# z's last quarter goes into the first rounds of the delta rule; GpSimd makes low parts; the second inverse lives in x's memory

## The reference, cut to what matters

```python
proj = h @ w_in
qkv, z, b_logit, a_logit = jnp.split(proj, ...)
qkv = silu(causal_depthwise_conv(qkv, conv_w))
...
o = chunked_gated_delta_rule(q, k, v, g, beta)      # chunks of 128 tokens, 16 heads
o = rms_norm(o, norm_w) * silu(z)
return o.reshape(bsz, t, GDN_V) @ w_out
```

## Time and profile before

| | us |
|---|---|
| median of 3 runs | 915.18 (913.97 to 915.21) |
| the profiled execution | 915.78 |
| its span, first to last instruction | 913.7 |
| PE busy | 879.3 (96%) |
| DVE busy | 698.0 (76%) |
| ACT busy | 510.4 (56%) |
| POOL busy | 46.6 (5%) |
| mean granted clock of TensorE | 0.977 |

### The profile page before, as it was taken

The page is one execution under the profiler, slowest core; times in us unless marked ns, Lnnn a source line. Parts: engine busy times, 40 slices in busy tenths (PEclk is TensorE's granted clock), DMA queues, the critical chain, the costliest instruction groups (busy, mean ns, idle before and its releaser), DMA issues.

```text
span 913.7 us, 16395 instructions
## 1 busy us (share of the span) xinstructions
PE 879.3 (96%) x6434; PEld 819.8 (90%) x6434; DVE 698.0 (76%) x1116; ACT 510.4 (56%) x729; POOL 46.6 (5%) x48
## 2 busy tenths in 40 slices
PE   5999999989897999999999999999999999999997
PEld 5999998779776999999997899999887799999995
DVE  5777889846756777777757677899999999956874
ACT  6598877546445555555545565333345675435642
POOL 0001110122010000000000000000001130001000
PEclk9999999979998999999999979999999999999999
DMA  8736664610465477777777525555455445555441
GB/s 255 231 116 184 194 178 139 174 53 2 161 208 184 139 251 251 253 248 247 255 248 263 184 77 185 178 184 185 156 173 178 138 139 185 185 190 173 140 143 46
DMA packets 139473, 161.55 MB, mean 177 GB/s; under 512 B 17155, under 2 KB 112283, under 8 KB 139419
## 3 DMA queue, kind: packets, MB, share of 16 engines
q1 hardware_dynamic: 139419, 160.80, 54.3%
HBM read 156.58 MB, written 4.21 MB: 176 GB/s over the span
## 4 chain that ended last, share of the span: by engine, by line
PE 73%; DVE 16%; ACT 5%; issue 2%; DMA 2%; SPq 1%; DVEq 0%; ACTq 0%
PE psum L480 22%; PE psum L482 22%; PE psum L481 22%; DVE w_lo L1376 5%; DVE cv L1819 3%; PE psum L765 3%; DMA w_raw<-in_sc_w_out_dram 1%; ACT w_hi L932 1%; DVE Tq L1604 1%; DVE outer L1602 1%; DVE cacc L1525 1%; PE psum L635 1%; ACT junk L965 1%; PE psum L869 1%; PE psum L647 1%
## 5 line engine op out<-in xcount | busy, mean ns | idle before, releaser
L1376 DVE TENSOR_TENSOR w_lo<-w_raw,w_hi 128x1024 fp32r<-128x1024 f32 x264 | 316.6, 1222 | 129.6 <-ACT w_hi L932 128.4
L932 ACT ACTIVATE w_hi<-w_raw 128x1024 fp32r<-128x1024 f32 x264 | 275.0, 1057 | 213.1 <-PE psum L482 166.6
L480 PE MATMUL psum<-hT_hi,w_hi 128*128 128x256 f32 x1216 | 349.9, 288 | 4.4 <-DVE w_lo L1376 3.8
L481 PE MATMUL psum<-hT_lo,w_hi 128*128 128x256 f32 x1216 | 346.9, 285 | 0.0
L482 PE MATMUL psum<-hT_hi,w_lo 128*128 128x256 f32 x1216 | 346.8, 285 | 0.0
L480 PEld LDWEIGHTS psum<-hT_hi,w_hi 128*128 128x128 f32 x1216 | 236.5, 195 | 5.9 <-issue 4.3
L481 PEld LDWEIGHTS psum<-hT_lo,w_hi 128*128 128x128 f32 x1216 | 236.5, 194 | 0.3 <-issue 0.2
L482 PEld LDWEIGHTS psum<-hT_hi,w_lo 128*128 128x128 f32 x1216 | 236.3, 194 | 0.0
L1819 DVE SCALAR_TENSOR_TENSOR cv<-aP,par,cv 128x256 f32<-128x256 f32 x240 | 106.8, 512 | 0.0
L480 PE MATMUL psum<-w_hi,hT_hi 128*128 128x512 f32 x224 | 91.3, 408 | 1.8 <-DVE w_lo L1376 1.8
L482 PE MATMUL psum<-w_hi,hT_lo 128*128 128x512 f32 x224 | 87.4, 390 | 0.0
(11 more groups left out here) (285 smaller groups left out, 1061.7 us busy)
## 6 DMA issues: line engine op xcount, KB each, us to landing
w_raw<-in_w_in_dram SPq DMA_DIRECT2D x44, 1024.0 KB, 5.0
w_raw<-in_sc_w_in_dram SPq DMA_DIRECT2D x32, 1024.0 KB, 7.3
w_raw<-in_gdn_w_in_dram SPq DMA_DIRECT2D x24, 1024.0 KB, 5.5
ada<-in_w_ada_dram SPq DMA_DIRECT2D x24, 512.0 KB, 4.7
w_raw<-in_gdn_w_out_dram SPq DMA_DIRECT2D x8, 1024.0 KB, 5.4
w_raw<-in_sc_w_out_dram SPq DMA_DIRECT2D x8, 1024.0 KB, 7.3
w_raw<-in_w_ret_out_dram SPq DMA_DIRECT2D x8, 1024.0 KB, 5.1
w_raw<-in_w_conv_out_dram SPq DMA_DIRECT2D x4, 1024.0 KB, 5.1
```

The source lines that it names most:

```text
L480: pe.matmul(o, l_hi, r_hi, start=start, stop=False, skip_group_check=True)
L481: pe.matmul(o, l_hi, r_lo, start=False, stop=False, skip_group_check=True)
L932: act.activation(w_hi[j % 2 * 2 + h][:, :, :], raw[slot][:, h * KH2:(h + 1) * KH2, :], ACT.Copy).then_inc(hi_ready, 1)
L1376: return dve.tensor_tensor(o, whole, hi.bitcast(F32), ALU.subtract)
```

## The change

1. Only chunks 0 to 5 of z run in the z stage (Z_AHEAD). The four halves of chunks 6 and 7 stand ahead of the level products of rounds 0 to 3, into banks 4 and 5; ScalarE's last silu of zo stands at the start of round 4.
2. GpSimd makes w_lo of the second halves of z's chunks 1 to 6 (POOL_LO). Who needs such a half waits for `lo_pool`; VectorE's `lo_ready` skips them and catches up at gdn_out's first half.
3. S[1] moves from w_raw's slot 2 into x's memory, and is cleared once xn is made. SP loads x again after the last V. gdn_out's chunks 2 and 3 are loaded right behind `blocks_home`, the row and chunks 4 and 5 after the last kdec, x, 6 and 7 after the last V.
4. The solve's shares are 10, 12, 12, 12, 16; the turn of its rows 0 to 23 is done before the last share, the other 8 rows after it.
5. k is turned after chunk 0 of z instead of after chunk 5, ahead of v.
6. The splits in the rounds: z's last half in round 0, gdn_out's (0,0), (0,1), (1,0), (1,1) in rounds 1 to 4, (2,0), (2,1), (3,0) in rounds 13 to 15 (before: (1,1) in 12, (2,0), (2,1), (3,0) in 15, 16, 17).

```diff
+SQ_ROWS = 24
-OUT_SPLITS = [(OUT_FROM, 1, 1), (OUT_FROM + 3, 2, 0), (OUT_FROM + 4, 2, 1), (OUT_FROM + 5, 3, 0)]
+Z_AHEAD = 6
+ROUND_SPLITS = [(0, "z", 7, 1), (1, "gdn_out", 0, 0), (2, "gdn_out", 0, 1), (3, "gdn_out", 1, 0), (4, "gdn_out", 1, 1),
+                (OUT_FROM + 1, "gdn_out", 2, 0), (OUT_FROM + 2, "gdn_out", 2, 1), (OUT_FROM + 3, "gdn_out", 3, 0)]
+POOL_LO = range(1, 7)
-        S1 = at("S1", o_raw + 16 * K, [P, VH, P])
+        S1 = at("S1", o_x, [P, VH, P])
...
+        def by_pool(g, h):
+            return h == 1 and g - FIRST["z"] in POOL_LO
+        def low_half(eng, g, h):
+            z0 = FIRST["z"]
+            if by_pool(g, h):
+                eng.wait_ge(lo_pool, g - z0 - POOL_LO[0] + 1)
+            else:
+                others = sum(by_pool(a, 1) for a in range(z0, g)) if g < z0 + COUNT["z"] else 0
+                eng.wait_ge(lo_ready, 2 * g + h + 1 - others)
...
-            for j in (0, 1, 3, 2):
-                if j == 3:
-                    blocks_home()
-                if j == 2:
-                    sp.wait_ge(vn_ready, NPAIR)
-                chunk(FIRST["gdn_out"] + j, j, wide_cols(gdn_w_out[0], j * (KH2 * P), 0))
+            out_chunk(0)
+            out_chunk(1)
+            blocks_home()
+            out_chunk(2)
+            out_chunk(3)
+            sp.wait_ge(kdec_ready, NPAIR)
             sp.dma_start(row[:, :], post_norm_w[0:1, :].to_broadcast([P, D])).then_inc(row_loaded, 16)
-            phase("gdn_out", four_pieces(gdn_w_out[0]), start=1, of=wide_cols)
+            out_chunk(4)
+            out_chunk(5)
+            sp.wait_ge(vn_ready, NPAIR)
+            for t in range(NT):
+                load_x(t)
+            out_chunk(6)
+            out_chunk(7)
...
             for r in range(ROUNDS):
+                if r < 4:
+                    c, h = Z_AHEAD + r // 2, r % 2
+                    if r == 0:
+                        pe.wait_ge(vb_ready, 2 * NPAIR - 1)
+                    wide_half(FIRST["z"] + c, h, 4, hT_hi, hT_lo, c % 2 * KH2, c % 2 == 0, c % 2 == 1)
                 if r < 8:
                     level5_w(r)
...
             for r in range(ROUNDS):
+                if r == 4:
+                    act.wait_ge(half_done, 4 + 2 * FIRST["gdn_out"])
+                    act.activation(zo[:, :, 3 * CW2:4 * CW2], psum[:, 4:6, :], ACT.Silu).then_inc(bank_free, 2)
...
-            pool.wait_ge(lo_ready, 2 * (FIRST["z"] + 7))
+            pool.wait_ge(xn_ready, 2 * NT)
             pool.memset(S[1], 0.0).then_inc(filled, 1)
+            def split_lo(c):
+                g = FIRST["z"] + c
+                s = g % 2 * 2 + 1
+                pool.wait_ge(hi_ready, 2 * g + 2)
+                pool.tensor_tensor(w_lo[s][:, :, :], raw[g % RING][:, KH2:KT, :], w_hi[s][:, :, :].bitcast(F32), ALU.subtract).then_inc(lo_pool, 1)
+            for c in POOL_LO:
+                split_lo(c)
+                if c == 4:
+                    (the memsets of Tc's side and S[0], with their waits)
...
-                    pool.wait_ge(bank_free, 4 + FIRST["gdn_out"])
+                    pool.wait_ge(half_done, 4 + 2 * FIRST["gdn_out"])
...
+            def turn_rows(a, b):
+                return dve.tensor_copy(Lq[:, :].rearrange("p (c r) -> p c r", r=BS)[:, :, a:b], Tq[:, :].rearrange("p (r c) -> p c r", c=BS)[:, :, a:b])
-                solve_share((8, 14, 14, 14, 12, 0, 0, 0)[c])
+                if c == 4:
+                    dve.wait_ge(solve_step, 2 * SQ_ROWS - 1)
+                    turn_rows(0, SQ_ROWS)
+                solve_share((10, 12, 12, 12, 16, 0)[c])
                 if c == 4:
                     dve.wait_ge(solve_step, 2 * (BS - 1) + 1)
-                    dve.tensor_copy(Lq..., Tq...).then_inc(sq_turned, 1)
+                    turn_rows(SQ_ROWS, BS).then_inc(sq_turned, 1)
```

More of the change, by code:

```diff
@@ L237, in build @@
         lnss_ready, ngk_ready, nb_ready = sem("lnss_ready"), sem("ngk_ready"), sem("nb_ready")
+        lo_pool = sem("lo_pool")
         nbT_ready, blocks_out, turned_out, solve_loaded = (
@@ L327, in chunk @@
             def chunk(g, slot, src, wait=True):
-                if wait:
+                if wait and isinstance(g, int):
+                    low_chunk(sp, g - RING)
+                elif wait:
                     sp.wait_ge(lo_ready, g * 2 - 2 * (RING - 1))
@@ L539, in wide_last, with wide_phase @@
                             mm.then_inc(first_done, 1)
-            def wide_phase(name, a_hi, a_lo, operand=None, beside=None):
+            def wide_phase(name, a_hi, a_lo, operand=None, beside=None, upto=None):
                 g0 = FIRST[name]
-                for c in range(COUNT[name]):
+                for c in range(upto or COUNT[name]):
                     g = g0 + c
@@ L688, in beside_z @@
                     squares(4 + c)
+                if c == 0:
+                    for n in range(2):
+                        for a in range(HG):
+                            mm = pe.transpose(bank(5 + n, P)[:, a, :], qkvT[:, KT + HG * n + a, 0:P], ident)
+                        mm.then_inc(k_turned, 1)
                 if 1 <= c < 5:
@@ L697, in beside_z @@
                         mm.then_inc(v_turned, 1)
[L698 to L704, removed]
+            wide_phase("z", hT_hi, hT_lo, beside=beside_z, upto=Z_AHEAD)
             def halves_of(e):
@@ L711, in level5_w @@
                 if n == 0:
[L712 removed]
+                    pe.wait_ge(bank_free, 4 + FIRST["z"] + Z_AHEAD)
                     pe.wait_ge(tc_loaded, 16 * (NB - 1))
@@ L936, in split_ahead, with chunks @@
                 split_hi(g0, i, j + 2, 0)
-            def chunks(name, each=None, unroll=False, ahead=0, held=0):
+            def chunks(name, each=None, unroll=False, ahead=0, held=0, upto=None):
                 g0 = FIRST[name]
                 def step(i):
-                    for j in range(4):
+                    for j in range(4 if upto is None else min(4, upto - 4 * i)):
                         if not unroll or ahead <= 4 * i + j < COUNT[name] - held:
@@ L1188, in _ @@
                         turn_y(p)
-                for at_r, j, h in OUT_SPLITS:
+                for at_r, name, j, h in ROUND_SPLITS:
                     if r == at_r:
-                        split_hi(FIRST["gdn_out"], 0, j, h)
+                        split_hi(FIRST[name], 0, j, h)
             turn_y(NPAIR - 1)
@@ L1381, in split_lo, with chunks @@
                     return
-                s = j % 2 * 2 + h
+                if isinstance(i, int) and by_pool(g0 + 4 * i + j, h):
+                    return
+                s, catch_up = j % 2 * 2 + h, 0
+                if isinstance(i, int) and (g0 + 4 * i + j, h) == (FIRST["gdn_out"], 0):
+                    dve.wait_ge(lo_pool, len(POOL_LO))
+                    catch_up = len(POOL_LO)
                 dve.wait_ge(hi_ready, i * 8 + (2 * (g0 + j) + h + 1))
-                part_lo(w_lo[s][:, :, :], raw[j % RING][:, h * KH2:(h + 1) * KH2, :], w_hi[s][:, :, :]).then_inc(lo_ready, 1)
-            def chunks(name, each=None, unroll=False, before_last=None, ahead=0, held=0):
+                part_lo(w_lo[s][:, :, :], raw[j % RING][:, h * KH2:(h + 1) * KH2, :], w_hi[s][:, :, :]).then_inc(lo_ready, 1 + catch_up)
+            def chunks(name, each=None, unroll=False, before_last=None, ahead=0, held=0, upto=None):
                 g0 = FIRST[name]
                 def step(i):
-                    for j in range(4):
+                    for j in range(4 if upto is None else min(4, upto - 4 * i)):
                         if not unroll or ahead <= 4 * i + j:
@@ L1480, in each @@
                         y_piece(n, b, 1, 0)
+                        if n == 0:
+                            for t in range(NT):
+                                dve.wait_ge(x_loaded[t], 32)
                         x_next(n, 0)
@@ L1705, in _ @@
                         turn_y(p)
-                for at_r, j, h in OUT_SPLITS:
+                for at_r, name, j, h in ROUND_SPLITS:
                     if r == at_r:
-                        split_lo(FIRST["gdn_out"], 0, j, h)
+                        split_lo(FIRST[name], 0, j, h)
             turn_y(NPAIR - 1)
```

37 lines of the change are left out of this document (23 added, 14 removed).

## The result

| | median us | runs, us | profiled span | mean clock |
|---|---|---|---|---|
| before | 914.70 | 913.97 to 915.21, 6 runs | 913.7 | 0.977 |
| after | 922.14 | 920.72 to 923.51, 6 runs | 920.4 | 0.973 |

The ratio is 1.0082, 95% interval 1.0069 to 1.0095: the change costs 7.4 us. The forecast was 925.0 us, with a range of 914.0 to 929.5.

The account below looks back on a forecast made before the run. It took TensorE (96% busy) as the bound, with VectorE's solve leading the z stage until 174.71. Round 6's +9.8 and the end's -0.2 gave +9.6 on 915.78 us, 925.4, stated as 925.0; range 914 to 929.5.

Parts of the forecast that it names:

- GpSimd stops VectorE for all but 0.25 us of its piece: In the solve, each 2.5 us GpSimd w_lo piece stalls VectorE 2.25 us; bounds 0 and 2.6.
- The two rivals without full stalls: During VectorE's solve: no meeting with GpSimd, 912.5 us, 18%; or a stall fixed at 1.05 us a piece, 918.2, 10%.
- The first copy's price: Turning rows 0 to 23 ahead of Tq costs VectorE three quarters of the copy's 2.10 us, +1.6 us.
- Tq at 182.1: At the solve's end on VectorE, Tq is ready at 182.1 instead of 172.6, a sum of +9.5 us.
- The trip of 7.7 us: From Tq through DRAM until Tc has landed takes 7.7 us, with a load landing 3.6 us after issue.
- From Tc to round 4, 12.3 + 2 to 2.5 us: TensorE needs 12.3 us from Tc's landing to round 4, plus 2 to 2.5 us for low clock after idling.
- the rival in which it stays low through rounds 0 to 3: TensorE's clock stays low after 11 us of idle, costing 5 to 6 us instead of 2.3: 928.5 us, 12%.
- Rounds 4 and 5 together: At full clock these level rounds sum to 7.2 us instead of 9.9, giving back 2.7 us.
- Round 6: The start of round 6 of the levels comes 9.8 us later than in the kernel before.
- The end of the rounds, -0.2: Out half (2,0) still starts at 249.9 as before, now waiting for yT_lo; booked -0.2 us, bounds +1.5 and -3.9.
- The bound of -3.9: Best case at the end of the rounds: idle and low clock both gone, (3,0)'s wait of 1.13 us kept.
- Edits at nothing: Removed z waits, k's earlier turn, moved memsets and loads, and other waits were booked as no gain or loss.

Follow-up runs that it names:

- e1: The kernel after with all low parts of z made by VectorE instead of GpSimd, the rest of the change kept: 914.57 us, ratio 1.0002.
- e2: The kernel before with only GpSimd's six low parts of z added: 920.25 us, ratio 1.0051.
- e3: The kernel before with only k's turn moved from after z's chunk 5 to after chunk 0: 912.76 us, ratio 0.9976.
- e4: The kernel after with gdn_out's (2,0) and (2,1) split one round earlier, in rounds 12 and 13: 919.13 us, ratio 1.0041.
- e5: e1 with gdn_out's (2,0) and (2,1) also split one round earlier, as in e4 (full name e5_both): 911.31 us, ratio 0.9969.
- e10_filled: e6_three_ahead with 11 unused ident-by-ident matmuls added on TensorE in rounds 0, 1 and 3: 906.57 us, ratio 0.9918.
- e6_three_ahead: e5 with three of z's four late halves issued before the first level product and (7,1) in round 2: 909.89 us, ratio 0.9954.
- e7: The kernel after with GpSimd's subtraction replaced by a one-input copy of the raw weights: 913.45 us, ratio 0.9995.

## Why the prediction was right

The mechanism was right, and the loss 2.4 us smaller than forecast (7.4 us, where 925.0 is 9.8 over the kernel before). By the prediction's own steps:

- **GpSimd stops VectorE for all but 0.25 us of its piece: right.** 2.11 to 2.23 us each for the five full ones, where 2.25 stood in the sum, and the first one net +1.2 as booked (1.36 of stall, 0.94 more of waiting for w_hi, less one low part of 1.14). e1 and e2 show the cause from both sides. The 0.25 us had been read off seven instructions of a different line; the prediction speaks of one long one, of 1530 ns, but the trace has a second, of 1509 ns at 706.54, one for each of GpSimd's two. So the rule carried over from 1.3 us pieces to 2.4 us ones. The two rivals without full stalls (912.5 and 918.2) fall by the six rows above.
- **The first copy's price: mis-sized.** The step "three quarters of the copy's 2.10 us: +1.6" came to 0.85. The 2.10 was itself a meeting with GpSimd's memset of S0, which e3 shows (1.15 without it). This is the largest error of a term, 0.8 us, and could have been seen in the trace of before: GpSimd's memset starts at 172.05, the copy at 172.62.
- **Tq at 182.1:** it came at 180.05: 0.8 for the copy, 0.3 for the five stalls, and 0.9 because this execution reached the z stage that much earlier (the six convolution instructions ahead of it start at 132.19, before at 133.07).
- **The trip of 7.7 us: mis-sized,** 7.0 to the first product; the landings took 2.8 us, not 3.6.
- **From Tc to round 4, 12.3 + 2 to 2.5 us: right,** 14.6 (187.10 to 201.74). The low clock covered the work from 187.1 to 192.2, half of which is 2.6 us lost, so the rival in which it stays low through rounds 0 to 3 is out. Rounds 4 and 5 together took 7.0 us (7.2 booked). Round 6 was 7.0 us later (208.75 against 201.79), not 9.8; the terms above, 0.8 + 0.3 + 0.9 + 0.7 + 0.2, make up that difference to 0.1 us.
- **The end of the rounds, -0.2: right,** 0. (2,0) waits for yT_lo as foreseen and is 7.03 us later than before, as round 6 is. The bound of -3.9 was a real possibility: with the splits one round earlier the same place gives 3.8 us (e4 against the kernel after, by the ratios) and 3.0 us (e5 against e1).
- **Edits at nothing.** K's turn was one: for it alone this is wrong, it gains 2.2 us (e3), of which 0.95 is the memset out of the copy's way and the rest is open. In the sum the 0.95 hid in the copy's term.

What the prediction didn't ask is why the change without its stalls gains nothing either (e1: 1.0002), although k's early turn, which is in it, gains 2.4 thousandths alone (e3). The late splits of (2,0) and (2,1) cost 3.3 thousandths of that (e5 against e1). With them mended e5_both (0.9969) is no better than k's early turn alone (0.9976): TensorE is idle 6.2 us before Tc, with the low clock behind it. Z's quarter in the rounds was never run by itself; of the kernels that have it, e10_filled, with the halves ahead and the gaps filled, is the only one that is faster than e3 beyond both intervals.

## What to carry to other kernels

Before work is handed to GpSimd, look at what VectorE does in that same stretch: beside two-input instructions, GpSimd's subtraction and its copy took nearly their own duration off VectorE, and 2.4 us on GpSimd to save 1.14 is a loss. A duration taken from the trace is a price only after looking at what ran beside it on the other engine. Where TensorE alternates with VectorE, a gain upstream can be given back by the clock, and a few useless matmuls in the gaps were worth 3 us here. A profile is one execution: compare its time with the median before reading the clock off it.

## What was not expected of the hardware

- A GpSimd memset (1.82 us) lengthens a VectorE copy of 128x1024 from 1.15 to 2.10 us, but not a two-input VectorE instruction (0.42 us beside it, 0.42 without).
- In e6_three_ahead TensorE waited 0.70, 0.47 and 1.53 us in rounds 0 to 3, and in the last of these waits its clock fell to the low level (1.2 GHz, 0.50 in the rows), from 190.1 to 200.4, though TensorE was fully busy in 192 to 200. In e10_filled, with 11 products in these places (22 instructions, 3.25 us together), the clock stayed at 1.00. The Trainium skill (TensorE: Matmul & The Clock Gate, Part 1: The HAM clock gate) says that the gate follows how busy the array has been lately, and the two traces agree in kind.
- GpSimd's copy of a 128x1024 tile is 1.04 us, its subtraction, with a second input, 2.39.
- TensorE's wait of 3.2 to 3.3 us ahead of (2,0) was followed by the low clock in the profiles of before, after, e1 and e7 (3.22 to 3.32 us) and not in those of e2 and e3 (3.21).
